# Decoder step: the sample tile's last mixing folded into four lanes, and the router's last prompt tiles fed without the shift

## The chip, the cores and the metric

The kernel runs on one core of one Trainium2 chip. The metric is device time in microseconds (us) of one execution. Three executions of the kernel before took 1709.33, 1714.53 and 1718.94 us; the median is 1714.53.

## The reference

One layer of a hybrid decoder for 1024 prompt tokens and 32 sample tokens (8 sequences of 4), model width 1024, all in f32. What matters for this change is the middle of the layer:

```python
merged = jax.nn.sigmoid(ga) * b_attn + jax.nn.sigmoid(gr) * b_lru
mix = merged @ p['w_out']
x = x + gt_a * _rms_norm(mix, p['g_post_mix'])
h2 = _rms_norm(x, p['g_pre_ffn']) * (1.0 + sc_f) + sh_f
f = _hier_moe(h2, p['w_router_group'], p['b_router_group'], ...)
x = x + gt_f * _rms_norm(f, p['g_post_ffn'])
```

`_rms_norm(x, g)` divides a row by the root of its mean square and multiplies by `g`. `_hier_moe` is a router and experts: `h2` times a router matrix of 36 columns (4 groups, 32 experts) plus a bias gives logits; the best group, and in it the best two of 8 experts, are chosen for each token; each expert computes `(silu(x @ w_gate) * (x @ w_up)) @ w_down` with two weights of 1024 x 512 and one of 512 x 1024 (2048 KB each), and the two results are added with the router's weights. `gt`, `sc` and `sh` come from a conditioning vector: one for the whole prompt, one for each of the 8 sample sequences.

## The kernel before, in words

The kernel is one program with an instruction list for each engine; every wait is written out as a semaphore. Tokens are split into three groups of columns (384, 384 and 288: the last has 256 prompt tokens and the 32 sample tokens) and nine tiles of rows, 0 to 7 of the prompt (128 rows) and 8, the sample tile (32 rows). Group g has the tiles 3g to 3g+2.

**Weights in a ring.** Steps of matrix products ("ga", "gr", "at", "lr" for the branches, "out" for the mixing) go through a ring of weights of 128 x 1024. SyncE (SP) loads one, ScalarE rounds it to the upper part (`round_weights`, L1186), VectorE subtracts to get the lower part (`split_weights`, L1645), and TensorE forms each product as three: upper x upper, upper x lower, lower x upper, in the form fp32r. The lower part is written over the raw weights.

**The last mixing.** The mixing of group g runs between the products of group g+1. That of the last group has nothing behind it: `mix(last, q)` for q = 0 to 7 (TensorE, definition above L2309, called behind the branches' products). A step takes two of eight slices of the contraction for one half of the 1024 columns: for each tile 2 x 3 products of 512 columns. Steps 0 to 3 make the left half, 4 to 7 the right half. VectorE meanwhile chooses experts for the six tiles of the groups before (`best`, L1767 to L1781, `choose`, L1786 to L1790), and in step 3 TensorE waits for that choice (`first_counts`) and for the order that VectorE makes from it (`early_places`, `first_order`), with which three experts are picked whose weights can be loaded at once (`eid0`, L1807).

**From the mix to the router.** For the last group, tile by tile: ScalarE squares the second half and takes a root (L1300, L1303); VectorE multiplies the mix by the gain (`last_half`, L1831), forms x1 (`last_x1`, L1839) and, with ScalarE's root of x1's squares (L1307, L1309), h2 (`last_h2`, L1846) and adds the shift B (L1847). TensorE turns h2 (`turn`, L2309), ScalarE copies it out of PSUM (`keep_turned`, L1237), TensorE multiplies it by the router matrix (`logits`), VectorE adds the bias (`keep_logits`, L1713) and chooses. In between TensorE multiplies matrices that nobody reads (`keep_warm`). The gains G1, A2 and B2 of the sample tile are rows of 1024 columns on 32 partitions, loaded by POOL (L917).

**From the router to the experts.** VectorE turns the choices into tables (L1868 to L1918): which token goes to which slot of 32 rows. When the first table is there, POOL gathers the token rows of two rounds from h2 in DRAM (`gather`, L925). A round of TensorE holds 128 slots, up to four experts side by side in four lanes of 32 rows: turn (L2428), gate, up, turn (L2463), down; all f32.

**Expert weights.** Three sets of buffers (gate, up, down) rotate. SP's queue is in order. It loads nine first weights (`first_weights`, L817) and then the rest (`expert_loads`, L841), each when the expert that had the buffer is done. Before the change the order around the router is:

```python
first_weights(0, ("gate", "up", "down"))
first_weights(2, ("gate",))
sp.wait_ge(step_done, STEP["out", GRP - 1, KC - 1] + 3)
first_weights(1, ("gate",))
... x1_store, h2_store of the last tiles
first_weights(1, ("up", "down"))
... waits for these stores and the turnings
first_weights(2, ("up",))
sp.wait_ge(tables, 4)
first_weights(2, ("down",))
```

Of the kernel before, what the change touches and what calls it, by code (L numbers as in the profile page):

```python
# [17 lines left out]
P = 128  # L18
# [45 lines left out]
XPAD = 3  # L64

# [28 lines left out]
LOW = 65536.0  # L94
assert [PLACE_RANK[n] for n in range(SETS)] == list(range(NE - SETS, NE))
# [80 lines left out]
def build(nc, I, O):  # L176
    ctx = ExitStack()
    with ctx:
# [143 lines left out]
        G1s, A2s, B2s = [at(n, [NS, D], m0[1] + i * D) for i, n in enumerate(("G1s", "A2s", "B2s"))]  # L322
# [79 lines left out]
        eprod0 = rtm("eprod0", [P, NE])  # L402
        rt, rt_end = 2 * big + KC * P, 2 * big + (RAW - 1 + UP) * KC * P
# [100 lines left out]
        idx_seen = sem("idx_seen")  # L504

        f_sum, f_pe, f_sq = sem("f_sum"), sem("f_pe"), sem("f_sq")
        y_added, y_pooled, st_out = sem("y_added"), sem("y_pooled"), sem("st_out")
# [4 lines left out]
        def row_sum(t):  # L512

            n = P if t < BLKS else NS
            if t in BY_PE:
                return ps[0:n, 2 * BY_PE.index(t) % 8:2 * BY_PE.index(t) % 8 + 2, :].rearrange("p h n -> p (h n)")
            return fy[0:n, t, 0, :]

# [22 lines left out]
        def tiles(g):  # L541

            return [(3 * g + j, j, P if 3 * g + j < BLKS else NS) for j in range(3)]

# [29 lines left out]
        def _(sp):  # L574
# [161 lines left out]
            def load_x(g):  # L736
# [3 lines left out]
                for t, j, n in tiles(g):  # L740
                    sp.dma_start(xh[j][0:n, :], I["x"][t * P:t * P + n, :]).then_inc(ld_xin, 16)

            def x1_store(t, j, n):
                sp.wait_ge(x1_ready, t + 1)
                sp.dma_start(x1_dram[t * P:t * P + n, :], x1[j][0:n, :]).then_inc(st_x1, 16)

            def h2_store(t, j, n):
                sp.wait_ge(h2_ready, t + 1)
                sp.dma_start(h2_dram[t * P:t * P + n, :], xh[j][0:n, :]).then_inc(st_h2, 16)
# [107 lines left out]
            sp.wait_ge(st_x1, 16 * TILES)  # L857
# [13 lines left out]
            for t in range(TILES):  # L871
                n = P if t < BLKS else NS
                if t in BY_POOL:
                    sp.wait_ge(y_pooled, BY_POOL.index(t) + 1)
# [8 lines left out]
        def _(pool):  # L883
# [1764 lines left out]
```

## Time and profile before

| | us |
|---|---|
| median of three runs (lowest, highest) | 1714.53 (1709.33, 1718.94) |
| the profiled execution, its own time | 1712.25 |
| span of the profiled execution | 1710.4 |
| TensorE busy | 1611.0 (94%) |
| VectorE, ScalarE, POOL busy | 753.6, 627.3, 128.1 |
| moved by DMA | 404.59 MB, mean 237 GB/s |

The profiled execution's own time is its span and 1.85 us around it. All times of the trace are counted from the start of the span. TensorE is shown as busy from the start of a product to its modelled end, so that two that follow each other overlap, and a plain f32 product is shown as two records; what a group of products costs is read from the starts. "What ended the idle time" of an engine is in brackets: idle us, then the work that it waited for.

### The profile page before, as it was taken

What the parts mean: (1) busy time and instruction counts of PE and PEld (TensorE: products, weight loads), DVE (VectorE), ACT (ScalarE), POOL (GpSimd) and SP (SyncE); (2) the same over time, 40 slices, a digit from 0 to 9 for tenths busy, and PEclk for the clock granted to TensorE, in tenths of its full rate; (3) what the DMA queues carried; (4) which work ended last, traced back from release to release, by engine and by line L of the source; (5) the groups of instructions that cost most, each with busy time, mean ns of one, the idle gap of its engine ahead of it and who ended that gap; (6) DMA issues with size and microseconds to landing.
All of it is one profiled execution on the core that took longest, in us unless ns stands there. A gap on an engine that the chain in (4) does not pass through costs nothing. (4 is left out here: it accounts for less than half of the span.)

```text
span 1710.4 us, 27124 instructions
## 1 busy us (share of the span) xinstructions
PE 1611.0 (94%) x11078; PEld 1159.1 (68%) x11078; DVE 753.6 (44%) x1402; ACT 627.3 (37%) x1191; POOL 128.1 (7%) x217
## 2 busy tenths in 40 slices
PE   6999988999999989999999999978998999999996
PEld 3889777888888889999999989762333333333343
DVE  3524347878888764453455455681000000000005
ACT  4525435665555663343444354321111111111112
POOL 0000011111111000000000030000000000000011
PEclk9999889999999999999999999999999999999998
DMA  9464561111111086373356564689999999999988
GB/s 375 167 199 143 172 199 50 54 42 53 54 54 53 27 297 216 127 271 124 124 185 234 185 196 159 247 321 376 417 392 428 428 424 424 406 406 392 408 323 313
DMA packets 96866, 404.59 MB, mean 237 GB/s; under 512 B 12215, under 2 KB 40151, under 8 KB 83800
## 3 DMA queue, kind: packets, MB, share of 16 engines
q1 hardware_dynamic: 84768, 380.23, 58.6%
q0 software_dynamic: 6960, 17.71, 2.7%
q10 hardware_dynamic: 5016, 4.93, 1.0%
q8 instruction: 88, 1.44, 0.3%
q14 instruction: 34, 0.28, 0.0%
HBM read 364.76 MB, written 44.32 MB: 239 GB/s over the span
## 5 line engine op out<-in xcount | busy, mean ns | idle before, releaser
L1186 ACT ACTIVATE wup<-wraw 128x1024 fp32r<-128x1024 f32 x120 | 126.7, 1059 | 272.2 <-PE ps L2002 234.4
L1645 DVE TENSOR_TENSOR wlow<-wraw,wup 128x1024 fp32r<-128x1024 f32 x120 | 146.8, 1224 | 158.9 <-ACT wup L1186 158.5
L2002 PE MATMUL ps<-wg,xT 128*32 128x512 f32 (+2 forms) x1072 | 156.1, 610 | 12.5 <-DMA wg<-w_gate 11.6
L2002 PE MATMUL ps<-wd,aT 128*32 128x512 f32 (+2 forms) x1072 | 148.5, 593 | 8.2 <-DMA wd<-w_down 6.8
L2002 PE MATMUL ps<-wu,xT 128*32 128x512 f32 (+2 forms) x1072 | 148.6, 594 | 4.2 <-DMA wu<-w_up 4.2
L2002 PE MATMUL ps<-h_up,wup 128*128 128x384 f32 (+1 forms) x384 | 126.1, 328 | 3.3 <-DVE wlow L1645 3.2
L2002 PE MATMUL ps<-h_up,wlow 128*128 128x384 f32 (+1 forms) x384 | 125.0, 326 | 0.0
L2002 PE MATMUL ps<-h_low,wup 128*128 128x384 f32 (+1 forms) x384 | 125.0, 325 | 0.0
L2002 PEld LDWEIGHTS ps<-wd,aT 128*32 128x32 f32 (+2 forms) x1072 | 47.1, 117 | 106.3 <-issue 104.6
L2002 PEld LDWEIGHTS ps<-wg,xT 128*32 128x32 f32 (+2 forms) x1072 | 44.9, 119 | 106.3 <-issue 103.1
L2002 PE MATMUL ps<-hp_up,wA_up 128*128 128x352 f32 x312 | 109.3, 350 | 0.6 <-DVE hp_low L1408 0.6
L1136 ACT ACTIVATE pp<-ps,ngm 128x256 f32<-128x256 f32 x128 | 59.5, 470 | 135.9 <-DVE skd L1530 120.4
L2002 PEld LDWEIGHTS ps<-wu,xT 128*32 128x32 f32 (+2 forms) x1072 | 46.0, 117 | 91.3 <-issue 89.4
L2002 PE MATMUL ps<-hp_up,wB_up 128*128 128x352 f32 x312 | 106.2, 340 | 1.6 <-ACT gB L1111 1.6
L2002 PE MATMUL ps<-hp_up,wA_low 128*128 128x352 f32 x312 | 102.3, 328 | 0.0
L2002 PE MATMUL ps<-hp_low,wA_up 128*128 128x352 f32 x312 | 102.2, 328 | 0.0
L2002 PE MATMUL ps<-hp_up,wB_low 128*128 128x352 f32 x312 | 100.8, 323 | 0.0
L2002 PE MATMUL ps<-hp_low,wB_up 128*128 128x352 f32 x312 | 100.7, 323 | 0.0
L1344 ACT ACTIVATE aT<-ps 128x512 f32<-128x512 f32 x20 | 11.9, 597 | 229.6 <-PE ps L2463 229.6
L1945 DVE TENSOR_TENSOR sgm<-sgm,ps 128x512 f32<-128x512 f32 x20 | 13.8, 688 | 168.4 <-ACT sgm L1336 168.4
L912 POOL COPY qst<-oT 64x128 f32<-64x128 f32 x128 | 57.8, 452 | 292.4 <-ACT oT L1165 288.0
L2002 PEld LDWEIGHTS ps<-h_up,wup 128*128 128x128 f32 x384 | 73.5, 192 | 4.5 <-issue 4.2
(402 smaller groups left out, 3291.9 us busy)
## 6 DMA issues: line engine op xcount, KB each, us to landing
wg<-w_gate SPq DMA_DIRECT2D x32, 2048.0 KB
wu<-w_up SPq DMA_DIRECT2D x32, 2048.0 KB, 15.9
wd<-w_down SPq DMA_DIRECT2D x32, 2048.0 KB, 14.3
wraw<-w_ga SPq DMA_DIRECT2D x24, 512.0 KB, 3.7
wraw<-w_gr SPq DMA_DIRECT2D x24, 512.0 KB, 3.6
wraw<-w_at SPq DMA_DIRECT2D x24, 512.0 KB, 3.5
wraw<-w_lr SPq DMA_DIRECT2D x24, 512.0 KB, 3.5
wraw<-w_out SPq DMA_DIRECT2D x24, 512.0 KB, 3.5
```

The source lines that it names most:

```text
L912: pool.tensor_copy(qst[half, u % 4, a, :], oT[half, u, i * P:(i + 1) * P]).then_inc(u_staged, 1)
L1136: act.activation(pp[:, s % 2, a, :], ps[:, 3 + s % 2, a * 2 * P:(a + 1) * 2 * P], ACT.Exp, bias=ngm[:, s % 2, a:a + 1], scale=SCALE, accum ...
L1186: act.activation(wup[n % UP][:, :, :], wraw[n % RAW][:, :, :], ACT.Copy).then_inc(w_rounded, 1)
L1344: act.activation(aT[:, :, :], ps[:, 6, :].rearrange("p (m c) -> p m c", c=P), ACT.Copy).then_inc(a_kept, 1)
L1645: V.tensor_tensor(wlow[n % RAW][:, :, :], wraw[n % RAW][:, :, :], wup[n % UP][:, :, :].bitcast(F32), ALU.subtract).then_inc(w_split, 1)
L1945: V.tensor_tensor(sgm[:, :], sgm[:, :], ps[:, 2, :], ALU.mult).then_inc(ch_moe, 1)
L2002: return pe.matmul(out, lhsT, rhs, start=start, stop=stop, skip_group_check=True)
```

## The change

The sample tile's part of the last mixing is computed as plain f32 from the raw weights, with the 32 rows in four lanes of 32 columns of the array: lane l makes the columns 128 l to 128 l + 127 of each half, and they land on partitions 32 l to 32 l + 31. The tile is then 128 x 256 instead of 32 x 1024, in x1, h2 and the gains. Row totals of squares are added over the lanes by a product with a matrix of zeros and ones (`same_row`). So that the raw weights live on, the lower parts of the last mixing go to buffers of their own. The two last prompt tiles are turned and multiplied by the router matrix before the shift B is added; B times the router matrix is computed once, ahead, and added to the bias (`br_shift`); B is added to h2 on VectorE afterwards. TensorE turns a tile before it multiplies the one before it, and is given fewer of the products that nobody reads. SP loads set 1's up weights together with its gate weights, stores the sample tile in four transfers, and issues the up weights of set 2 and the down weights of set 1 only when POOL has issued both first gathers (`pool_done`).

```diff
         G1p, A2p, B2p = [at(n, [P, D], t4 + i * D) for i, n in enumerate(("G1p", "A2p", "B2p"))]
-        G1s, A2s, B2s = [at(n, [NS, D], m0[1] + i * D) for i, n in enumerate(("G1s", "A2s", "B2s"))]
+        G1s, A2s, B2s = [at(n, [P, FD], m0[1] + 2 * KC * CW - (3 - i) * FD) for i, n in enumerate(("G1s", "A2s", "B2s"))]
+        wlow_last = [at(f"wlow_last{i}", [P, KC, P], m0[1] + i * KC * P, F32R) for i in range(UP)]
...
+                        sp.dma_start(lane_rows(x1_dram[SEQ:TOK, :], l), lane_part(x1[j], l)).then_inc(st_x1, 16)
+
+            def h2_store(t, j, n, ready=1):
+                sp.wait_ge(h2_ready, t + ready)
+                if t < BLKS:
+                    sp.dma_start(h2_dram[t * P:t * P + n, :], xh[j][0:n, :]).then_inc(st_h2, 16)
+                else:
+                    for l in range(LANES):
+                        sp.dma_start(lane_rows(h2_dram[SEQ:TOK, :], l), lane_part(xh[j], l)).then_inc(st_h2, 16)
 
             sp.wait_ge(proj_done, N_PROJ)
...
@@ -821,16 +860,17 @@
             first_weights(0, ("gate", "up", "down"))
             first_weights(2, ("gate",))
             sp.wait_ge(step_done, STEP["out", GRP - 1, KC - 1] + 3)
-            first_weights(1, ("gate",))
+            first_weights(1, ("gate", "up"))
             for t, j, n in tiles(GRP - 1):
                 x1_store(t, j, n)
-            for t, j, n in tiles(GRP - 1):
-                h2_store(t, j, n)
-            first_weights(1, ("up", "down"))
-            sp.wait_ge(st_x1, 16 * TILES)
-            sp.wait_ge(st_h2, 16 * TILES)
+            for j, ready in ((2, 2), (0, 5), (1, 5)):
+                h2_store(*tiles(GRP - 1)[j], ready)
+            sp.wait_ge(st_x1, 16 * (BLKS + LANES))
+            sp.wait_ge(st_h2, 16 * (BLKS + LANES))
             sp.wait_ge(h2_turned, 2 * TILES)
+            sp.wait_ge(pool_done, 1)
             first_weights(2, ("up",))
+            first_weights(1, ("down",))
             sp.wait_ge(tables, 4)
             first_weights(2, ("down",))
...
             for a, h, ts in ((0, 0, G1s), (1, 0, A2s), (0, 2, B2s)):
-                for b in range(NB):
-                    pool.dma_start(ts[NT * b:NT * (b + 1), :].rearrange("p (h n) -> p h n", h=2),
-                                   mod_dram[a, h:h + 2, 1 + b:2 + b, :].rearrange("h r n -> r h n").broadcast_to([NT, 2, 512])).then_inc(ld_samples, 16)
+                for l in range(LANES):
+                    for hh in range(2):
+                        pool.dma_start(ts[NS * l:NS * (l + 1), P * hh:P * (hh + 1)],
+                                       bc(mod_dram[a, h + hh, 1:1 + NB, P * l:P * (l + 1)].unsqueeze(1), (NB, NT, P))).then_inc(ld_samples, 16)
+            pool.dma_start(same_row[:, :], I["same_row"]).then_inc(ld_samples, 16)
 
             pool.wait_ge(tables, 1)
-            pool.wait_ge(st_h2, 16 * TILES)
...
             gather(1)
+            pool.sem_inc(pool_done, 1)
             pool.wait_ge(xg_used, 1)
             gather(2)
...
                 mix_piece(last, q)
+                if q == 5:
+                    act.wait_ge(lg_done, 3 * last)
+                    act.wait_ge(fold_pe, 1)
+                    act.activation(h2T[:, :, :], bc(ps[:, 7, SHIFT:SHIFT + KC].unsqueeze(2), (P, KC, P)), ACT.Copy).then_inc(rt_exp, 1)
             act.wait_ge(mix_sum, last + 1)
...
+                    act.wait_ge(fold_pe, 3)
+                    act.activation(tst[:, 3, j:j + 1], ps[:, 7, FOLD:FOLD + 1], ACT.Sqrt, bias=eps[:, :], scale=1.0 / D).then_inc(mix_root, 1)
+            def x1_square(j):
+                t, w = 3 * last + j, 2 * span(3 * last + j)
                 act.wait_ge(x1_ready, t + 1)
-                act.activation(junk[0:n, :], x1[j][0:n, :], ACT.Square, accum_out=tst[0:n, 4, j:j + 1]).then_inc(x1_sq, 1)
-                act.wait_ge(x1_sq, t + 1)
-                act.activation(tst[0:n, 5, j:j + 1], tst[0:n, 4, j:j + 1], ACT.Sqrt, bias=eps[0:n, :], scale=1.0 / D).then_inc(x1_root, 1)
...
-                dve.wait_ge(ld_xin, 48 * GRP)
-                V.scalar_tensor_tensor(x1[j][0:n, :], x1[j][0:n, :], tst[0:n, 3, j:j + 1], xh[j][0:n, :], ALU.mult, ALU.add).then_inc(x1_ready, 1)
+                dve.wait_ge(ld_xin, 16 * (BLKS + LANES))
+                V.scalar_tensor_tensor(x1[j][:, 0:w], x1[j][:, 0:w], tst[:, 3, j:j + 1], xh[j][:, 0:w], ALU.mult, ALU.add).then_inc(x1_ready, 1)
 
             def last_h2(j):
-                t, j, n = tiles(last)[j]
+                t, w = 3 * last + j, 2 * span(3 * last + j)
                 dve.wait_ge(x1_root, last + j + 1)
-                k(V.reciprocal(tst[0:n, 5, j:j + 1], tst[0:n, 5, j:j + 1]))
+                k(V.reciprocal(tst[:, 5, j:j + 1], tst[:, 5, j:j + 1]))
                 dve.wait_ge(x1_ready, t + 1)
-                k(V.scalar_tensor_tensor(xh[j][0:n, :], x1[j][0:n, :], tst[0:n, 5, j:j + 1], A2(t)[0:n, :], ALU.mult, ALU.mult))
-                V.tensor_tensor(xh[j][0:n, :], xh[j][0:n, :], B2(t)[0:n, :], ALU.add).then_inc(h2_ready, 1)
+                V.scalar_tensor_tensor(xh[j][:, 0:w], x1[j][:, 0:w], tst[:, 5, j:j + 1], A2(t)[:, 0:w], ALU.mult, ALU.mult).then_inc(h2_ready, 1)
+
+            def last_shift(j):
+                t, w = 3 * last + j, 2 * span(3 * last + j)
+                dve.wait_ge(h2_ready, TILES)
+                if t < BLKS:
+                    dve.wait_ge(h2_turned, 2 * t + 2)
+                V.tensor_tensor(xh[j][:, 0:w], xh[j][:, 0:w], B2(t)[:, 0:w], ALU.add).then_inc(h2_ready, 1)
 
             last_half(0)
             last_x1(0)
             last_half(1)
             last_x1(1)
             last_h2(0)
+            dve.wait_ge(fold_pe, 2)
+            k(V.tensor_tensor(br_shift[:, :], ps[:, 6, 0:NG + NE], brt[:, :], ALU.add))
             last_half(2)
             last_x1(2)
             last_h2(1)
             last_h2(2)
+            last_shift(2)
+            last_shift(0)
+            last_shift(1)
             keep_logits(last, 0, (6, 0))
             dve.wait_ge(lg_kept, 3 * last + 1)
...
+                    out, cols = ps[:, mix_bank(g, hf, j), :], slice(j * P, j * P + rows)
                     for kk in range(2):
                         k = 2 * kp + kk
+                        if t == BLKS:
+                            for l in range(LANES):
+                                ins = mm(ps[NS * l:NS * (l + 1), mix_bank(g, hf, j), 0:P], merged[g % 2][:, k, cols],
+                                         w_raw[:, kk, P * l:P * (l + 1)], k == 0, k == KC - 1)
+                            continue
                         mm(out, m_up[g % 2][:, k, cols], w_up[:, kk, :], k == 0, False)
                         mm(out, m_up[g % 2][:, k, cols], w_low[:, kk, :], False, False)
...
 
                 t, j, n = tiles(g)[j]
-                pe.wait_ge(h2_ready, t + 1)
+                pe.wait_ge(h2_ready, t + 1 + (t == BLKS))
+                if t == BLKS:
+                    pe.transpose(ps[:, at, 0:P], xh[j][:, part * P:(part + 1) * P], ident[:, :]).then_inc(h2_turned, 1)
+                    return
                 for k in range(4):
...
+            def row_totals(col, parts):
+
+                for i, s in enumerate(parts):
+                    ins = mm(ps[:, 7, FOLD + col:FOLD + col + 1], same_row[:, :], tst[:, s, 2:3], False, i + 1 == len(parts))
+                ins.then_inc(fold_pe, 1)
 
             def turn_along(g, o, q):
...
                 ins.then_inc(order_pe, 1)
+                for k in range(KC):
+                    ins = mm(ps[:, 7, SHIFT + k:SHIFT + k + 1], B2p[0:1, k * P:(k + 1) * P], ident[0:1, 0:1], True, True)
+                ins.then_inc(fold_pe, 1)
 
             for q in range(KC):
                 mix(last, q, {0: first_counts, 2: first_order} if q == 3 else {})
+            pe.wait_ge(rt_exp, 1)
             pe.wait_ge(rt_ready, 2)
             rank(0, 3 * last)
             pe.wait_ge(early_ready, 3)
-            keep_warm(44)
+            pe.wait_ge(mix_kept, 6 * last + 3)
+            pe.wait_ge(mix_sq, 6 * last + 3)
+            chunk_sum(ps[:, 6, 0:NG + NE], lambda k: h2T[:, k, :], lambda k: wr[:, k, :]).then_inc(fold_pe, 1)
+            pe.wait_ge(ld_samples, 16 * 3 * 2 * LANES + 16)
+            pe.wait_ge(mix_sq, 6 * last + 6)
+            row_totals(0, (0, 1))
+            keep_warm(14)
             pe.wait_ge(lg_kept, 3 * last)
-            for j in range(3):
+
+            def turn_last(j):
                 pe.wait_ge(mix_kept, 6 * last + 3 + j)
                 pe.wait_ge(mix_sq, 6 * last + 3 + j)
                 if j == 2:
                     pe.wait_ge(h2T_ready, 2 * 3 * last + 2)
                 turn(last, j, 0, (4, 0, 4)[j])
                 turn(last, j, 1, (5, 2, 5)[j])
-                keep_warm(5)
+
+            def logits_last(j):
                 if j:
                     pe.wait_ge(mix_kept, 6 * last + 4 + j)
                     pe.wait_ge(mix_sq, 6 * last + 4 + j)
                 if j == 2:
                     pe.wait_ge(lg_kept, 3 * last + 1)
                 logits(last, j, ((6, 1, 6)[j], 64 * (j // 2)), (h2T, h2Tb, h2T)[j])
-                if j < 2:
-                    keep_warm(6)
+
+            turn_last(0)
+            keep_warm(4)
+            pe.wait_ge(x1_sq, TILES)
+            row_totals(1, (4,))
+            turn_last(1)
+            logits_last(0)
+            turn_last(2)
+            logits_last(1)
+            logits_last(2)
```

## Rows read from the trace of the kernel before

**Rows 1.** The page: the chain that ended last, shares of the span by engine

```profile
PE 23%; DMA 8%; DVE 2%; issue 1%; ACT 0%; SPq 0%; POOLq 0%; POOL 0%; DVEq 0%; ACTq 0%
```

**Rows 2.** Chain of work in order of time (start us, us, what)

```profile
1148.90 4.72 DMA xg<-h_dram,slot_from
...
1448.42 16.29 DMA wu<-w_up
```

**Rows 3.** Busy us by stretch: the five engines, PE clock, DMA share, GB/s

```profile
1151.00:1152.00 1.00, 0.94 (x16) 0.91 (x16) 0.93 (x5) 0.00 (x0) 0.91 (x1) 1.00 0.82 188
1152.00:1153.00 1.00, 0.35 (x5) 0.11 (x2) 0.96 (x2) 0.00 (x0) 0.00 (x0) 1.00 0.64 164
1148.00:1170.00 22.00, 18.19 (x170) 7.84 (x172) 8.44 (x23) 3.07 (x4) 4.68 (x4) 1.00 0.71 257
1170.00:1464.00 294.00, 272.16 (x2008) 95.02 (x2000) 24.13 (x35) 37.39 (x59) 22.29 (x22) 0.98 1.00 418
1464.00:1640.00 176.00, 173.54 (x1272) 59.55 (x1272) 15.86 (x23) 24.04 (x38) 14.13 (x14) 1.00 0.98 402
```

**Rows 4.** Timeline of TensorE (start us, us, what), last mixing

```profile
1077.61 0.40 PE L2002 MATMUL ps<-wup,m_up 128*32 128x512 f32 x1
...
1079.00 0.39 PE L2002 MATMUL ps<-wup,m_up 128*128 128x512 f32 x1
...
1090.43 0.27 PE L2002 MATMUL ps<-ohs,ubf 128*128 128x32 bf16 x4 [1.49 <-DVE ohs L1790]
...
1093.63 0.50 PE L2002 MATMUL ps<-wup,m_up 128*128 128x512 f32 x1
...
1110.48 0.69 PE L2002 MATMUL ps<-ohs,ubf 128*128 128x32 bf16 x21
```

**Rows 5.** Timeline of TensorE: products in four lanes, 64 and 512 columns

```profile
234.96 1.10 PE L2002 MATMUL ps<-wslab,cE 128*32 128x64 f32 x64
...
1155.57 7.08 PE L2002 MATMUL ps<-wg,xT 128*32 128x512 f32 x64 [0.75 <-ACT xT L1330]
```

**Rows 6.** Timeline of TensorE's weight loads: router product, turning of 32 rows

```profile
1118.37 1.86 PEld L2002 LDWEIGHTS ps<-wr,h2T 128*128 128x128 f32 x16 [0.47 <-ACT h2T L1237]
...
1125.62 0.57 PEld L2309 LDWEIGHTS ps<-ident,xh 32*128 32x128 f32 x8 [0.21 <-issue]
```

**Rows 7.** Timeline of ScalarE: squares of the mix and of x1

```profile
1107.97 0.60 ACT L1300 ACTIVATE junk<-ps 128x512 bf16<-128x512 f32 x1 [8.71 <-PE ps L2002]
...
1111.97 1.04 ACT L1307 ACTIVATE junk<-x 128x1024 bf16<-128x1024 f32 x1
```

**Rows 8.** Timeline of VectorE, last mixing to the router

```profile
1092.32 0.24 DVE L1798 TENSOR_SCALAR lower<-key,kcol 128x32 bf16<-128x32 f32 x1
...
1113.88 1.28 DVE L1846 SCALAR_TENSOR_TENSOR xh<-x,tst,A2p 128x1024 f32<-128x1024 f32 x1
1115.20 1.23 DVE L1847 TENSOR_TENSOR xh<-xh,B2p 128x1024 f32<-128x1024 f32 x1
1116.35 0.67 DVE L1831 TENSOR_TENSOR x<-ps,G1s 32x512 f32<-32x512 f32 x1
...
1127.84 0.17 DVE L1767 COPY lg<-lg 128x8 f32<-128x8 f32 x1
```

**Rows 9.** Timeline of SyncE's queue: up weights of set 2

```profile
1130.73 0.34 SPq L817 DMA_DIRECT2D wu<-w_up  x1
```

**Rows 10.** Timeline of POOL: the first two gathers

```profile
1148.90 1.38 POOL L925 DMA_INDIRECT xg<-h_dram,slot_from  x1 [126.50 <-DVE slot_from L1918]
1150.58 1.32 POOL L925 DMA_INDIRECT xg<-h_dram,slot_from  x1 [0.30 <-issue]
```

**Rows 11.** Timeline of TensorE: two waits for expert weights

```profile
1324.66 3.11 PE L2002 MATMUL ps<-wg,xT 128*32 128x512 f32 x16 [4.41 <-DMA wg<-w_gate]
...
1384.06 2.37 PE L2002 MATMUL ps<-wd,aT 128*64 128x512 f32 x10 [2.24 <-DMA wd<-w_down]
```

**Rows 12.** Busy us by stretch, behind the longer of these waits

```profile
1326.00:1328.00 2.00, 2.00 (x15) 0.57 (x11) 0.00 (x0) 0.00 (x0) 0.00 (x0) 0.50 1.06 447
```

More of the change, by code:

```diff
@@ L64 @@
 XPAD = 3
+FD = D // LANES
 def worst_overflow():
@@ L94 @@
 LOW = 65536.0
+SHIFT = 384
+FOLD = 12 * NE
 assert [PLACE_RANK[n] for n in range(SETS)] == list(range(NE - SETS, NE))
@@ L543, in tiles, with span, prompt_width, low_part @@
             return [(3 * g + j, j, P if 3 * g + j < BLKS else NS) for j in range(3)]
+        def span(t):
+            return D // 2 if t < BLKS else FD // 2
+        def prompt_width(g):
+            return min(width(g), SEQ - CUT[g][0])
+        def low_part(n):
+            return wlow_last[n % UP] if n >= STEP["out", GRP - 1, 0] else wlow[n % RAW]
         def bank(key):
@@ L1299, in _ @@
                 act.wait_ge(step_done, STEP["out", last, KC - 1] + 1 + j)
-                act.activation(junk[0:n, 0:512], ps[0:n, mix_bank(last, 1, j), :], ACT.Square,
-                               accum_out=tst[0:n, 1, j:j + 1]).then_inc(mix_sq, 1)
-                act.wait_ge(mix_sq, 6 * last + 4 + j)
-                act.activation(tst[0:n, 3, j:j + 1], tst[0:n, 1, j:j + 1], ACT.Sqrt, bias=tst[0:n, 2, j:j + 1],
-                               scale=1.0 / D).then_inc(mix_root, 1)
-            for t, j, n in tiles(last):
-                act.wait_ge(x1_ready, t + 1)
-                act.activation(junk[0:n, :], x1[j][0:n, :], ACT.Square, accum_out=tst[0:n, 4, j:j + 1]).then_inc(x1_sq, 1)
-                act.wait_ge(x1_sq, t + 1)
-                act.activation(tst[0:n, 5, j:j + 1], tst[0:n, 4, j:j + 1], ACT.Sqrt, bias=eps[0:n, :], scale=1.0 / D).then_inc(x1_root, 1)
-                if j == 1:
-                    for part in range(2):
-                        keep_turned(last, 0, part, (4, 5)[part])
+                w = span(t)
@@ new lines, in x1_square, with x1_sqrt @@
+            def x1_square(j):
+                t, w = 3 * last + j, 2 * span(3 * last + j)
+                act.wait_ge(x1_ready, t + 1)
+                act.activation(junk[:, 0:w], x1[j][:, 0:w], ACT.Square, accum_out=tst[:, 4, j:j + 1]).then_inc(x1_sq, 1)
+            def x1_sqrt(j, total):
+                act.activation(tst[:, 5, j:j + 1], total, ACT.Sqrt, bias=eps[:, :], scale=1.0 / D).then_inc(x1_root, 1)
+            for j in range(2):
+                x1_square(j)
+                act.wait_ge(x1_sq, 3 * last + j + 1)
+                x1_sqrt(j, tst[:, 4, j:j + 1])
@@ L1313, in _ @@
+            keep_turned(last, 0, 0, 4)
+            x1_square(2)
+            keep_turned(last, 0, 1, 5)
+            act.wait_ge(fold_pe, 4)
+            x1_sqrt(2, ps[:, 7, FOLD + 1:FOLD + 2])
             for j in (1, 2):
@@ L2292, in mix @@
                 for t, j, rows in tiles(g):
-                    out, cols = ps[0:rows, mix_bank(g, hf, j), :], slice(j * P, j * P + rows)
+                    out, cols = ps[:, mix_bank(g, hf, j), :], slice(j * P, j * P + rows)
                     for kk in range(2):
                         k = 2 * kp + kk
+                        if t == BLKS:
+                            for l in range(LANES):
+                                ins = mm(ps[NS * l:NS * (l + 1), mix_bank(g, hf, j), 0:P], merged[g % 2][:, k, cols],
+                                         w_raw[:, kk, P * l:P * (l + 1)], k == 0, k == KC - 1)
+                            continue
                         mm(out, m_up[g % 2][:, k, cols], w_up[:, kk, :], k == 0, False)
```

82 lines of the change are left out of this document (55 added, 27 removed).

## The prediction

> **What bounds the kernel now.** I read the chain of work that ended last first. By its shares TensorE and DMA carry it [rows 1], and read in order of time it runs through three stretches. Up to the first gather of token rows it is a chain of small steps on TensorE, VectorE and ScalarE: POOL issues the gather at 1148.90 and it takes 4.72 us to land [rows 2]. From there to 1464.71 it goes through expert weights: the last link of that kind is an up load that takes 16.29 us from issue to landing [rows 2]. After that it is TensorE alone up to the last round.
>
> The busy times by stretch tell what such a long load means. From 1170 to 1464 the DMA engines are busy for a share of 1.00 at 418 GB/s, while TensorE is busy for 272 of 294 us; from 1464 to 1640 TensorE is busy for 173.5 of 176 [rows 3]. So for some 300 us the transfers are the bound, and what sets the end is when the stream of weights gets through. Just ahead of it, from 1148 to 1170, the DMA share is 0.71 [rows 3]: 6.4 us of DMA time idle. An earlier gather (I call the start of the first one T, 1148.90 now) moves the end only if the stream moves with it. That is the question of this change; the two parts of the answer follow.
>
> **Part 1: what the change takes from T.** *The mixing.* A step q of the last mixing has 18 products, six of them for the 32 sample rows: from 1077.61 to 1079.00, 1.39 us [rows 4]. After it there are 2 x 4 lanes of plain f32 at 128 columns. Such lanes run side by side: 64 records (8 sets of four lanes, each product shown as two records) take 1.04 us at 64 columns, 0.13 a set, and 7.08 us at 512 columns, 0.885 a set [rows 5]. At 128 columns a set lies between 0.13 and a quarter of 0.885, 0.22. I take 0.22, as the rows at 64 and 512 columns are in no proportion and the larger is the safer: 0.44 a step, 0.95 saved.
>
> In steps 0 to 2 that buys little. TensorE already stands still for 1.49 us in step 3, for VectorE's choice of experts (1088.94 to 1090.43) [rows 4]. VectorE's work there is one unbroken row that starts with the weights of step 0, so it moves by 0.95 only, to 1089.48. TensorE comes to that wait at 1085.93: the stall grows to 3.55 us. From there: second tile 1.40, sample tile 0.44, then the next VectorE result (its last step starts at 1092.32 and takes 0.24 [rows 8], less 0.95: 1091.6), and then the eight new one-row products that turn B. The trace has none with one row. Nearest are eight products with 128 x 128 weights, 1.86 us, and eight turnings of 32 rows, 0.57 [rows 6]. I take 1.86: the weights have 128 columns in both, and f32 products load them twice while turnings do so once. (The Trainium skill, "TensorE: Matmul & The Clock Gate", Step-by-step, has the time of a weight load go by its columns and not by its rows, which gives 1.86 too; the 32-row rows of this trace, at 0.07 a load against 0.12, speak for less. With 0.57, T and the forecast come 1.3 earlier.) Step 4 so starts at 1093.6, where it starts now (1093.63) [rows 4]. Steps 4 to 6 save 3 x 0.95, and the first tile of step 7 ends about **2.95 us earlier**.
>
> *The end of the stage*, counted from ScalarE's first square of the second half (1107.97) [rows 7]. Now x1's first square starts at +4.00 [rows 7], the first product of h2 at +5.91, and the last two tiles' choice at +19.87 [rows 8]. After the change:
> - TensorE ends the mixing at +1.55 (+2.51 now, less 0.95) [rows 4], counts ranks (0.55), makes the router's product of the shift (1.86) and the row totals (four records of 0.116, 0.46): +4.5. ScalarE, in order, waits there for the sample tile's total before x1's square: +4.85 in place of +4.00. VectorE had 0.2 us in hand, so h2 of the first tile starts at +6.5 and ends at +7.8.
> - VectorE now leaves out the addition of B there (1.23), and the sample tile's half and x1 shrink from 0.67 and 1.27 to some 0.25 and 0.40 (128 and 256 columns by the 0.67 for 512) [rows 8]. Tile two's h2 ends at +10.35, not +13.07.
> - TensorE: turning to +11.3, router product one to +13.15, sample turning, product two to +15.35, product three (0.7) +16.0. The sample's own router product is no shorter; it has the same form.
> - VectorE: sample h2 and its shift (0.7), two shifts of 1.23 to +13.7, logits and choice of the first tile (2.2), logits of the other two: +16.4. It and TensorE end together; a little off either buys nothing.
>
> +16.4 against +19.87 is 3.45. With 2.95, T comes **6.4 us earlier**, at 1142.5. The steps between that choice and the gather are unchanged.
>
> Costs that I set at nothing: nine more sample transfers on SP's queue, 0.34 us each [rows 9], issued while it waits for x1 and h2; POOL's 24 sample loads stay 24, plus one, and are issued right behind the second group's mixing, long before they are read; ScalarE's broadcast of B in step 5 (1024 columns, 1.04 us as its square of x1, while the engine idles 8.71 us ahead of +0 [rows 7]); Without that cover each would show in full. The last rows of h2 are ready at +13.7, 1118.7 on the clock, 24 us before T.
>
> **Part 2: what it gives back.** Two of the nine first weight loads, up of set 2 and down of set 1, are now issued ahead of the router's end, the later at 1130.73 [rows 9], and run while it works. Now SP holds them until both gathers are issued. They are 2 x 2048 KB: at 418 GB/s 10.0 us of transfers moved from before T, where the engines then stand idle, to behind T, where the stream is the bound. Every later weight load is queued behind them on SP. Against that they fill holes. POOL issues at T and T+1.68, the second for 1.32 [rows 10], so SP is let go at T+3.0, and I let data flow from T+4.0 on. The idle sum of 6.4 begins 0.9 us ahead of T (1148); from there, idle are 3.0 us up to T+2.1, and 0.18 and 0.36 of the next two by their shares, 0.82 and 0.64 [rows 3]: 3.5 us. Behind it nothing stops: with the down load of set 2 some 15 us of transfers are queued, and the next experts' loads come at about T+14, when the first gate products are done. So 10.0 - (6.4 - 3.5) = **7.1 us given back**.
>
> Sum: -6.4 + 7.1 = **+0.7 us**, no change. The profiled execution took 1712.25 us (span 1710.4) and would take 1713.0; the median of the three runs shown is 2.3 above it, so the forecast is 1714.53 + 0.7 = 1715.2. Ends of the terms: B's turnings -1.3, lane sets -0.7, the hole filling 1.0 either way, the tail of the stage 1.5 either way: 1711 to 1718.
>
> **Rivals.** *A, the stream is not the bound* that I take it for: the held loads vanish in idle DMA time and all 6.4 arrive: 1708.1. For it, TensorE is on the chain for most of those 300 us, and 1.00 is a share of packet time, not proof that nothing could be faster. Against it, 22 us of TensorE's idle time in that stretch, and the rate of 418 GB/s throughout.
>
> *B, slower: the clock.* The stall in step 3 grows to 3.55 us. Here an idle of 2.24 us left TensorE at a granted clock of 1.00, one of 4.41 us was followed by 0.50, that is 1.2 GHz, where 16 records took 3.11 us and not 1.77 [rows 11, 12]. That is 1.3 us lost on 16 records; the clock may stay low for more of them, 3.0 at most if it does so for 6 us. I take 2.0, all on the path as steps 4 to 7 are TensorE's: 1717.2. [...] The same page of the Trainium skill (HAM oscillation) has an idle engine fall to half rate and the products after the gap run slow, which is this rival; the trace agrees at 4.41 us.
>
> *C, the lanes do not run together* where all four share one set of weights: then the fold doesn't do what it says. Eight records of 128 columns in a row are as long as one set of 512, 0.885; a step grows by 0.4, T gains some 0.2 only, and 7.1 is given back: 1721.4. Against it, the same lane form in every expert round.
>
> **Chances.** Forecast 0.60, A 0.16, B 0.13, C 0.05, the rest (a table later, other contention) 0.06. The range takes A's value and most of B in: 1708 to 1720. A measurement of this kernel can tell about 0.5%, 8.6 us, from no change. No case alone crosses it: A lies 6.4 under, C 6.9 over. What crosses is a case with an error of its own: 0.08 faster, 0.07 slower, 0.85 the same.
>
> **What would show it.** In the profile after: sample products of a step in about 0.45 us; a hole of 3.5 us on TensorE in step 3, clock 1.00 behind it; first gather near 1142.5; a DMA share near nought for some 9 us ahead of it and 1.00 from T+4 on; the last long wait for weights still ends at about 1465. If that wait ends near 1458, A is right and the account of part 2 wrong. If the first gather is not 5 to 8 us earlier, part 1 is.

## The result and the profile after

Over 20 executions each, the kernel after took 1719.15 us (1713.78 to 1725.21) and the kernel before 1714.35 us (1709.33 to 1719.39); the ratio is 1.0032, 95% interval 1.0022 to 1.0042. So the change costs some 5 us, where +0.7 was forecast. That is inside the range of 1708 to 1720, by 0.9 us, and inside 0.5% of no change, but outside the noise: the sign is a small loss. The profiled execution took 1717.99 us, its span 1716.1 us, 5.7 more than before.

The chain of waits of the kernel after, around the first gather (start us, us, what), answers to [rows 2]:

```profile
1147.39 8.81 DMA xg<-h_dram,slot_from
...
1170.04 12.45 DMA wg<-w_gate
```

T is 1147.39, only 1.5 earlier, and 0.5 of this has come about ahead of the change (see the mark, below). The gather itself takes 8.81 us in place of 4.72.

Busy us by stretch, kernel after (PE, PEld, DVE, ACT, POOL; then PE clock, DMA share, GB/s), answers to [rows 3]:

```profile
1090.00:1096.00 6.00, 6.00 (x28) 4.95 (x32) 1.14 (x6) 0.00 (x0) 0.00 (x0) 0.50 0.31 109
1137.00:1149.00 12.00, 9.09 (x79) 7.31 (x77) 11.13 (x26) 0.93 (x1) 1.38 (x1) 0.85 0.02 7
1148.00:1170.00 22.00, 15.45 (x113) 6.84 (x114) 6.30 (x18) 2.58 (x4) 3.08 (x3) 0.77 0.89 355
1151.00:1168.00 17.00, 11.01 (x68) 3.92 (x72) 2.82 (x11) 1.88 (x2) 0.99 (x1) 0.70 1.00 423
1170.00:1464.00 294.00, 277.43 (x2024) 95.46 (x2020) 24.82 (x37) 36.52 (x58) 23.26 (x23) 0.97 1.00 418
1464.00:1640.00 176.00, 174.23 (x1296) 60.01 (x1290) 15.85 (x23) 24.73 (x39) 14.11 (x14) 1.00 0.98 403
```

Three things are to be seen. For 12 us ahead of the gather the DMA engines now do nothing (share 0.02). Behind it they are full, and the long stretch is full at 418 GB/s as before. And TensorE ran at half clock from 1090 to 1096, in step 3 of the last mixing, where before it had full clock.

Timeline of TensorE, kernel after, answers to [rows 4, 5]: a sample part of the mixing, the stall in step 3, the turnings of B and what follows, and the first round:

```profile
1084.36 0.64 PE L2083 MATMUL ps<-wraw,merged 128*32 128x128 f32 x16
...
1089.16 0.27 PE L2083 MATMUL ps<-ohs,ubf 128*128 128x32 bf16 x4 [2.56 <-DVE ohs L1861]
1089.35 3.57 PE L2083 MATMUL ps<-ident,B2p 1*128 1x1 f32 x16
1092.85 0.80 PE L2083 MATMUL ps<-wup,m_up 128*128 128x512 f32 x1
1093.44 0.63 PE L2083 MATMUL ps<-wlow_last,m_up 128*128 128x512 f32 x1
...
1095.71 0.82 PE L2083 MATMUL ps<-wraw,merged 128*32 128x128 f32 x16
1096.47 0.18 PE L2083 MATMUL ps<-lower,ubf 32*128 32x32 bf16 x1
1096.58 0.51 PE L2083 MATMUL ps<-wup,m_up 128*128 128x512 f32 x1
...
1156.24 1.97 PE L2543 MATMUL ps<-ident,xg 128*128 128x128 f32 x8 [5.39 <-DMA xg<-h_dram,slot_from]
1158.96 9.75 PE L2083 MATMUL ps<-wg,xT 128*32 128x512 f32 x64 [0.75 <-ACT xT L1398]
```

The first gate products take 9.75 us, not 7.08, as TensorE stood 5.39 us for the gather and came back at half clock (granted 0.70 in the mean from 1151 to 1168).

The end of the stage: ScalarE's and VectorE's timelines, kernel after, answer to [rows 7, 8]:

```profile
1109.08 0.60 ACT L1355 ACTIVATE junk<-ps 128x512 bf16<-128x512 f32 x1 [4.19 <-PE ps L2083]
...
1113.98 1.05 ACT L1367 ACTIVATE junk<-x 128x1024 bf16<-128x1024 f32 x1
```

```profile
1115.67 1.28 DVE L1917 SCALAR_TENSOR_TENSOR xh<-x,tst,A2p 128x1024 f32<-128x1024 f32 x1
...
1120.64 2.35 DVE L1924 TENSOR_TENSOR xh<-xh,B2p 128x1024 f32<-128x1024 f32 x2
...
1125.46 0.17 DVE L1838 COPY lg<-lg 128x8 f32<-128x8 f32 x1
...
1133.18 0.25 DVE L1962 TENSOR_SCALAR ohrank<-ps,row 128x32 bf16<-128x32 f32 x1 [0.94 <-PE ps L2083]
```

POOL and SyncE's queue, kernel after, answer to [rows 9, 10]:

```profile
1147.39 1.38 POOL L967 DMA_INDIRECT xg<-h_dram,slot_from  x1 [126.84 <-DVE slot_from L1999]
1149.08 1.32 POOL L967 DMA_INDIRECT xg<-h_dram,slot_from  x1 [0.31 <-issue]
```

```profile
1098.75 0.37 SPq L856 DMA_DIRECT2D wg<-w_gate  x1
...
1148.55 0.36 SPq L856 DMA_DIRECT2D wu<-w_up  x1
1149.69 4.89 SPq L856 DMA_DIRECT2D wd<-w_down  x2
```

The held up load is issued at 1148.55. That is 1.16 us behind T and ahead of the record of the second gather (1149.08), though the signal stands behind both in POOL's list: its flight lies beside both gathers.

The last long wait for weights ends, in the kernel after and then in the kernel before (timeline of TensorE):

```profile
1468.96 7.07 PE L2083 MATMUL ps<-wu,xT 128*32 128x512 f32 x64 [0.22 <-DMA wu<-w_up]
```

```profile
1465.04 7.07 PE L2002 MATMUL ps<-wu,xT 128*32 128x512 f32 x64 [0.92 <-DMA wu<-w_up]
```

So 3.9 of the 5.7 us have come about by then; the rest comes in the end stage, from there 247.1 us in place of 245.4.

### The profile page after: what moved, and what is told of

Read it like the earlier page. It is cut to its first block, busy times and chain, and to the rows that moved or that the text cites. A ratio compares the mean times of both kernels' runs of the same rounds, so it can differ in the third digit from the quotient of the medians.

```text
span 1716.1 us, 27261 instructions
## 1 busy us (share of the span) xinstructions
PE 1613.9 (94%) x11137; PEld 1160.3 (68%) x11137; DVE 750.1 (44%) x1403; ACT 627.1 (37%) x1192; POOL 127.5 (7%) x218
## 4 chain that ended last, share of the span: by engine, by line
PE 77%; DVE 9%; DMA 8%; ACT 3%; issue 2%; SPq 0%; DVEq 0%; ACTq 0%; POOLq 0%; POOL 0%
PE ps L2083 74%; DMA wd<-w_down 4%; PE ps L2543 1%; DMA wada<-w_ada 1%; DVE olst L1648 1%; PE ps L2295 1%; DVE mx L1596 1%; DMA wraw<-w_at 1%; DMA wlate<-w_ada 1%; DMA wg<-w_gate 1%; PE ps L2578 1%; DMA fy<-y_dram 1%; DMA xg<-h_dram,slot_from 1%; DVE xc L1638 0%; PE ps L2398 0%
## 5 line engine op out<-in xcount | busy, mean ns | idle before, releaser
L1713 DVE TENSOR_TENSOR wlow<-wraw,wup 128x1024 fp32r<-128x1024 f32 x112 | 136.9, 1224 | 153.8 <-ACT wup L1229 153.4
L2083 PE MATMUL ps<-wg,xT 128*32 128x512 f32 (+2 forms) x1072 | 159.6, 624 | 9.4 <-DMA wg<-w_gate 8.5
L2026 DVE TENSOR_TENSOR sgm<-sgm,ps 128x512 f32<-128x512 f32 x20 | 13.7, 687 | 168.7 <-ACT sgm L1404 168.7
## 6 DMA issues: line engine op xcount, KB each, us to landing
wu<-w_up SPq DMA_DIRECT2D x32, 2048.0 KB, 15.7
```

What stands on the lines that cost most here:

```text
L1713: V.tensor_tensor(low_part(n)[:, :, :], wraw[n % RAW][:, :, :], wup[n % UP][:, :, :].bitcast(F32), ALU.subtract).then_inc(w_split, 1)
L2026: V.tensor_tensor(sgm[:, :], sgm[:, :], ps[:, 2, :], ALU.mult).then_inc(ch_moe, 1)
L2083: return pe.matmul(out, lhsT, rhs, start=start, stop=stop, skip_group_check=True)
```

## Experiments

"The hold" is SP's wait for POOL's signal (`pool_done`) ahead of two weight loads. Executions differ ahead of the change as well, so every T is read from a mark that the change does not touch: the last product of the recurrent and attention branches. In the view of one tile (durations min/median/max, first and last start) before, and after:

```profile
L2002 PE MATMUL ps<-o_up,wlow x16: 289/296/297, 1050.3 to 1068.4; 128*128 128x288 f32 x16
```

```profile
L2083 PE MATMUL ps<-o_up,wlow x16: 289/295/297, 1049.8 to 1067.9; 128*128 128x288 f32 x16
```

The last start is the mark. In the table T and the end of the last long wait are counted from it; "slow" is the length of the stretch at half clock in step 3; "gather" is the flight of the first one; "DMA idle" is what the DMA shares of the 80 us from 30 to 110 behind the mark leave (in eight stretches of 10 us, 1 less the share). One profile each.

| kernel | median us | ratio to before | T | gather | slow | DMA idle | last wait |
|---|---|---|---|---|---|---|---|
| before | 1714.35 | 1 | 80.5 | 4.72 | none | 10.2 | 396.6 |
| after | 1719.15 | 1.0032 (1.0022–1.0042) | 79.5 | 8.81 | 6.8 | 15.8 | 401.1 |
| before, with the hold | 1720.91 | 1.0050 (1.0030–1.0069) | 80.5 | 9.78 | none | 18.1 | 402.8 |
| after, no hold | 1714.95 | 1.0007 (0.9991–1.0022) | 79.2 | 6.68 | 6.8 | 11.8 | 399.0 |
| after, longer hold | 1720.74 | 1.0042 (1.0025–1.0059) | 79.5 | at most 4.83 | 6.8 | 16.9 | 401.4 |
| after, B early | 1714.67 | 1.0013 (0.9996–1.0031) | 75.9 | 8.87 | 3.4 | 13.8 | 397.1 |
| no hold, B early | 1709.66 | 0.9965 (0.9951–0.9979) | 73.9 | 6.34 | none | 8.1 | 390.1 |
| the same, stores first | 1709.47 | 0.9972 (0.9958–0.9986) | 73.8 | 4.75 | none | 4.5 | 387.4 |
| after, kept warm | 1718.81 | 1.0022 (1.0008–1.0036) | 78.5 | 8.88 | 6.8 | 13.7 | 398.9 |
| before, one more input | 1714.80 | 0.9997 (0.9982–1.0012) | 80.6 | 4.71 | none | 9.9 | |

The ratios are the ones to compare: the medians of 6 to 12 executions are coarse, and a ratio and its medians differ by up to 2 us (B early with the hold: 2.2 us over the kernel before by the ratio, 0.3 by the medians). Single profiles are coarse too: in the kernel before with one more input, the products that end the last wait of the kernel before start at 397.8, 1.2 later, with the same instructions.

The last wait follows the DMA idle time. Against the kernel before, the hold alone adds 7.9 us of it and the last wait comes 6.2 later; the kernel after adds 5.6 and 4.5, the longer hold 6.7 and 4.8, no hold 1.6 and 2.4. In the three kernels with B early the last wait lies another 3 to 4 us lower than their idle time alone would have it, which is not explained.

**The hold alone, in the kernel before.** The theory is that the stream of weights is the bound, and the hold takes transfers out of it; the rival is that its price is what it does to the gather and to TensorE.

```diff
-            first_weights(1, ("up", "down"))
+            first_weights(1, ("up",))
...
+            sp.wait_ge(gathers_out, 1)
             first_weights(2, ("up",))
+            first_weights(1, ("down",))
```

(`gathers_out` is raised by POOL behind `gather(1)`.)

> The kernel before with one thing of the change: the up load of set 2 and the down load of set 1 wait on SP until POOL has issued both first gathers. Nothing else moves, so the first gather's start stays at about 1148.9. Theory S (the weight stream sets the end, and loads that are moved behind the gather push it): 10.0 us of transfers moved, some 2.5 to 2.9 us of idle DMA time filled, so 7 us slower than before, 1.004. Rival G (the stream is not the bound; what costs in the changed kernel is the longer flight of the gather, 8.8 us in place of 4.7, and TensorE's low clock after it): 4 to 6 us slower, with the wait for the gather longer and the last long weight wait not moved. Rival N (the held loads vanish in idle time): no change.

Measured: +6.5 us by the medians, last long wait 6.2 later. Busy us by stretch, in 50 us around the router, of this kernel and of the kernel before:

```profile
1122.00:1172.00 50.00, 36.33 (x332) 23.84 (x333) 28.44 (x99) 7.06 (x13) 3.69 (x3) 0.83 0.64 251
```

```profile
1122.00:1172.00 50.00, 40.11 (x386) 24.59 (x384) 29.41 (x100) 7.18 (x13) 4.68 (x4) 0.93 0.79 309
```

The share falls from 0.79 to 0.64, which is 7.5 us of transfers pushed behind this stretch: the size of the loss. The last wait, 300 us later, has moved by nearly the whole amount. But TensorE stands and runs slow here too (gather 9.78 us), and the next experts' load is issued 21.6 us behind T in place of 14.0, which could move the last wait as well. So the two are not apart by this kernel alone; the kernel with the longer hold parts them.

**The hold taken out of the kernel after.**

```diff
             sp.wait_ge(h2_turned, 2 * TILES)
-            sp.wait_ge(pool_done, 1)
             first_weights(2, ("up",))
```

> The changed kernel without the hold: the same two loads go out as soon as the h2 stores have landed. Theory S: the DMA engines work through from 1099 to the gather without a gap of more than 2 us, the first gather starts as in the changed kernel (1147.4), and the 7 us come back: 1712 us, 0.996 of the changed kernel and 0.999 of the kernel before. Rival G gives 4 us at most, if the gather is as short as before. Rival N: as the changed kernel, 1719.

Measured: 4.2 us less by the medians, level with before. That is between the 7 us of the one theory and the 4 us of the other and decides nothing. The hold's price is not wholly back, since without it SP is still late. Its queue in this kernel:

```profile
1112.90 0.34 SPq L856 DMA_DIRECT2D wu<-w_up  x1
...
1140.79 0.35 SPq L856 DMA_DIRECT2D wu<-w_up  x1
```

The load waits for h2's stores. They are issued 3 us later from the mark than before, as they now come behind the additions of B, and they land near 1140, 13.7 us behind the last issue (1127.08) in place of 6.7 (1124.01 to 1130.73 before): the up load of set 1 now stands ahead of them in the queue. The hold hid this second lateness.

**A longer hold**, until TensorE has read the first gathered rows.

```diff
-            sp.wait_ge(pool_done, 1)
+            sp.wait_ge(xg_used, 1)
```

> The changed kernel with a longer hold: the two loads wait until the first gather has landed and TensorE has turned it. The gather then flies alone, 4.7 us as before, and TensorE waits for it some 4 us less. Theory S: the gather's flight is beside the point; the DMA engines idle about 6 us more behind the gather, less the 1.5 us that POOL's third gather fills, so 3 to 5 us slower than the changed kernel. Rival G: 4 us faster than the changed kernel.

Measured: 1.6 us over the kernel after by the medians, with intervals that overlap; the last wait is 0.3 later. The theory had 3 to 5 us more, its rival 4 us less. The timeline of TensorE, then SP's queue:

```profile
1149.11 1.16 PE L2543 MATMUL ps<-ident,xg 128*128 128x128 f32 x8 [1.36 <-DMA xg<-h_dram,slot_from]
```

```profile
1151.12 0.36 SPq L856 DMA_DIRECT2D wu<-w_up  x1
```

The gathered rows are used 4.83 us behind T (1144.28), not 8.85: the slow gather was the held loads' doing. But they start 6.84 behind T, not 1.16. The next experts' load is issued 15.7 us behind T (1159.99), not 21.5. Four us won at the gather against 5.7 lost by the stream come to nought or a small loss. If the gather's delay and the late load behind it alone were the price, this kernel would have been the better one. What did not shrink is the idle time of the DMA engines, 16.9 us against 15.8. So the stream is the larger part, by less than the theory said.

**B turned ahead of the stall in step 3**, not behind it.

```diff
             def first_counts():
+                pe.wait_ge(lg_kept, 3 * last)
+                for k in range(KC):
+                    ins = mm(ps[:, 7, SHIFT + k:SHIFT + k + 1], B2p[0:1, k * P:(k + 1) * P], ident[0:1, 0:1], True, True)
+                ins.then_inc(fold_pe, 1)
                 pe.wait_ge(rt_ready, 1)
...
-                for k in range(KC):
-                    ins = mm(ps[:, 7, SHIFT + k:SHIFT + k + 1], B2p[0:1, k * P:(k + 1) * P], ident[0:1, 0:1], True, True)
-                ins.then_inc(fold_pe, 1)
```

> The changed kernel with B's eight one-row turnings put ahead of the wait for the first choice of experts in step 3, into TensorE's stall of 2.56 us, instead of behind it. Theory: they took 3.5 us there; the stall hides most of them, the first gather starts 2.5 to 3.5 us earlier (near 1144.5), the early weight loads too, and as the stream follows the gather the whole kernel is 2.5 to 3.5 us faster than the changed one, 1716. If the low clock behind the stall is what costs, it goes too, as TensorE is never idle for long: up to 2 us more. Rival: the loads' start does not matter and the stream stays: no change.

Measured: 4.5 us less than after by the medians, T 3.6 earlier from the mark. Timeline of TensorE:

```profile
1085.15 1.94 PE L2083 MATMUL ps<-ident,B2p 1*128 1x1 f32 x16
1087.78 0.28 PE L2083 MATMUL ps<-ohs,ubf 128*128 128x32 bf16 x4 [0.69 <-DVE ohs L1861]
```

The turnings fill the stall, of which 0.69 us is left, and cost 1.94 us at full clock, as against 3.57 in the kernel after. In this execution the clock still fell behind it, for 3.4 us (1087.83 to 1091.25).

**Both: no hold, and B early**, the two edits together.

> The changed kernel with both: no hold, and B's turnings ahead of the wait. The first gather starts near 1142.5 as with the turnings alone. Without the hold the last long wait for weights came 319.8 us after the gather's start, with it 321.2 to 321.6, before the change 316.1. Theory S with the buffers as a second limit (once all nine first loads have landed, no more can start until the gate products of the first round are done): 319.8 after 1142.5, so 1.5 us faster than the turnings alone and 2 us faster than the kernel before, 1712 to 1713. If no low clock follows the gather, 316 after 1142.5: 1709. Rival: the hold is needed once the gather is early, since the loads then run into it: no faster than the turnings alone, 1715.

Measured: 1709.66 us, ratio 0.9965, faster than before and after. Here the clock stayed up through step 3; of this kernel, by stretch:

```profile
1089.00:1097.00 8.00, 7.31 (x57) 5.64 (x56) 6.28 (x30) 2.54 (x5) 0.00 (x0) 1.00 0.61 215
```

Up to this point the kernel is the same as the last one, and differs from it in the profile only by the clock: 3.4 us at half rate there, none here. Step 4's first product, in this kernel and in the last one (timeline of TensorE):

```profile
1094.92 0.48 PE L2082 MATMUL ps<-wup,m_up 128*128 128x512 f32 x1
```

```profile
1091.65 0.50 PE L2083 MATMUL ps<-wup,m_up 128*128 128x512 f32 x1
```

It starts 23.6 us behind the mark (1071.3) here and 25.1 (1066.5) there. That prices this low stretch: 1.5 us. T is 2.0 apart (75.9 and 73.9), as the clock goes its own way behind the mixing too: the ranks keep VectorE waiting 0.94 us there and 0.26 here. From T to the last wait it is 316.2 us here, as in the kernel before (316.1): here all that T gains arrives.

**Stores first**: set 1's up load goes behind the stores of x1 and h2 as well.

```diff
-            first_weights(1, ("gate", "up"))
+            first_weights(1, ("gate",))
...
                 h2_store(*tiles(GRP - 1)[j], ready)
+            first_weights(1, ("up",))
```

> The last one with the up load of set 1 issued behind the stores of x1 and h2 instead of ahead of them, as in the kernel before. Theory: in the changed kernel the stores queue behind 10 MB of weights and land only near 1140, so that the two last loads cannot start before that; with the stores ahead they land some 5 us earlier, the DMA engines have no hole, and all loads are through before the gather. Gather alone again (4.7 us in place of 6.7 to 8.8), no low clock after it: 316 us from the gather to the last long wait, 1709, the fastest so far. Rival: the place of the stores does not matter, as the last one: 1712.

Measured: the same time within the interval (ratio 0.9972), though in the profile the last wait is another 2.7 us earlier. Around the router, by stretch, and TensorE's timeline at the gather:

```profile
1122.00:1172.00 50.00, 36.34 (x346) 21.78 (x345) 26.93 (x92) 4.62 (x8) 4.69 (x4) 0.88 0.90 350
```

```profile
1149.57 1.16 PE L2544 MATMUL ps<-ident,xg 128*128 128x128 f32 x8 [1.33 <-DMA xg<-h_dram,slot_from]
1151.48 7.07 PE L2083 MATMUL ps<-wg,xT 128*32 128x512 f32 x64 [0.75 <-ACT xT L1398]
```

The share is 0.90, hardly any weights fly beside the gather (share 0.50 in its flight, before 0.40), it takes 4.75 us, TensorE waits 1.33 us, and the first gate products take 7.07 us, as at full clock before. The stores land 62.1 us behind the mark, as before (62.3), and not at 67.0 as in the last kernel: so their lateness was for the most part the place of the up load. One profile is too little to claim the 2.7 us.

**Kept warm**: 16 products that nobody reads in the stall of the kernel after, to hold the clock.

```diff
             def first_counts():
-                pe.wait_ge(rt_ready, 1)
                 pe.wait_ge(mg_sig, len(SIGMOIDS))
                 pe.wait_ge(mg_out, len(SCALED))
+                keep_warm(16)
+                pe.wait_ge(rt_ready, 1)
```

> The changed kernel with 16 products that nobody reads in TensorE's stall of step 3, and B's turnings still behind the stall. It parts the two costs that moving the turnings took away together. If the low clock (0.50 from 1089.2 to 1096.1 in the changed kernel's profile) is the larger one: turnings in 1.9 us and not 3.5, second tile of the step 1.4 and not 2.6, the first gather 3 us earlier, near 1144.3, the kernel 1717 to 1718 in the median since only some executions have the low clock there. If the clock is beside the point: 1719 as the changed kernel.

Measured: 0.3 us under the kernel after, which is nothing, with T 1.0 earlier from the mark. By stretch:

```profile
1091.00:1092.00 1.00, 1.00 (x10) 1.00 (x10) 0.97 (x3) 0.00 (x0) 0.00 (x0) 1.00 0.96 369
1092.00:1093.00 1.00, 1.00 (x8) 1.00 (x7) 0.75 (x4) 0.00 (x0) 0.00 (x0) 0.61 1.02 383
1093.00:1099.00 6.00, 6.00 (x29) 4.22 (x30) 0.98 (x6) 1.64 (x3) 0.00 (x0) 0.50 0.10 30
```

The stall was down to 0.80 us and the clock came through it, but then fell at 1092.23, 1.3 us behind the start of B's turnings (1090.92) and while they ran, and stayed low for 6.8 us all the same. So here the fall came without a long idle, and filling the stall did not cure it. What did help was to have the turnings elsewhere.

**One more input.** From the last long wait to the end it is 246.6 to 247.7 us in every kernel made from the one after and in the kernel after, and 245.4 and 245.8 before and before with the hold. About a microsecond of it is the load of the results (10.3 to 11.1 us; before, and before with the hold, 9.35 to 9.38). A suspect was the added table `same_row`, which moves what lies in DRAM. The kernel before got it as an unused input.

```diff
+        "same_row": (q % NS == k % NS).astype(np.float32),
```

> The kernel before with only the 64 KB input that the change adds, never read. In the changed kernel and all kernels made from it the last loads of the results take 10.3 to 10.5 us and not 9.4, and the end from the last long weight wait is 1 to 2 us longer, 246.6 to 247.4 in place of 245.4. If that comes from where tensors lie in DRAM, it shows here: 1 to 1.5 us slower than the kernel before. If not, no change, 1714.4.

Measured: no change. The chain of waits shows the load of the results at its old length; this kernel first, then the kernel after:

```profile
1673.90 9.37 DMA fy<-y_dram
```

```profile
1674.43 10.52 DMA fy<-y_dram
```

The input is not the cause. What is stays open.

## Why the prediction was right, and where it was wrong

That 1719.15 lies in the range owes as much to its width as to the account: the sum's own ends were 1711 to 1718. Part 2 was right in kind and too high by 1.7 us, part 1 was 4.9 us off.

**The stream as the bound: right.** Rival A (all of an earlier T arrives, the held loads vanish) is out: the last wait ends at 1468.96, not near 1458, the hold alone costs 6.5 us, and the last wait moves with the idle time of the DMA engines. Of the 7.1 us given back, 5.4 show between T and the last wait (321.57 us against 316.14). The end stage adds 1.8, a term that the sum did not have; 1.1 of it is the load of the results above. -1.5, +5.4 and +1.8 make +5.7, by which the span grew. In between, two steps of that account were off and met each other: SP was let go at T+1.16 and not at T+3.0, and so data flowed earlier; but the gather then took 8.81 us, TensorE came late and slow, and the next experts' load was issued at T+21.5, not T+14 (1168.93 in the chain of waits; in the kernel with the stores first it is 1158.76, T+14.0). The DMA share from 1168 to 1171 was 0.59: the hole that was thought closed.

**Part 1: T 6.4 earlier was forecast, 1.5 measured** (1.0 from the mark). Of the 4.9 missing, 4.1 are there by ScalarE's first square (1109.08; the forecast has 1105.0):
- *The clock, some 3 us, is the step that failed.* VectorE's result came at 1089.16, forecast 1089.48. From there to step 4's first product (1096.58) the forecast has 4.1 us and the trace 7.4. The turnings of B took 3.5 us, not 1.86, the second tile 2.86 (1092.85 to 1095.71), not 1.40: both are twice their length, at a granted clock of 0.50. This is rival B, at its upper end of 3.0 us. It was given 0.13, for a stall of 3.55 us; the stall was 2.56, and the clock fell at 1089.31, 0.15 us behind its end. The Trainium skill, "TensorE: Matmul & The Clock Gate", HAM oscillation, says that the engine falls after idling and that what follows is slow; the trace agrees, and shows more: in the kernel kept warm the fall came during the turnings, not right behind an idle. What the rival lacked is the turnings: eight products of one column, right behind the stall, so that they ran at half clock. Whether they also bring the fall about is not shown. In this kernel and in the one with the longer hold it came 0.04 and 0.03 us ahead of the first turning, without the hold 0.2 us and kept warm 1.3 us behind its start. With them ahead of the stall, in three kernels, the low stretch was 3.4 us, none and none.
- *The order in step 3.* The forecast puts the turnings behind VectorE's next result. The kernel has them ahead of the second tile. By the forecast's own prices that comes to the same (1093.5 in place of 1093.6), but it is why they stand right behind the stall.
- *The lane sets, 1.0 us.* The sample part of a step takes 0.77 us (the period of a step went from 4.19 to 3.56, and 4.19 - 1.39 + 0.77 = 3.57), not 0.44. Steps 4 to 6 so give 0.33 less each. The forecast took a set's price from the long runs of one shape; here 16 records take 0.57 us from first start to the next product, 0.28 a set of four, above both ends of the stated bracket (0.13 and 0.22), and some 0.2 go at the two changes between the forms. The stall in step 3 was shorter for it (2.56 against 3.55), which is why steps 0 to 2 cost nothing more. Rival C (lanes one after the other, which has a set at 0.885 us) is out.
- *B's turnings at full clock: right.* 1.94 us with B early, forecast 1.86. A weight load of one row costs as much as one of 128 rows; the other end, 0.57 us from 32-row turnings, was wrong. The Trainium skill, "TensorE: Matmul & The Clock Gate", Step-by-step, has a load go by its columns and not by its rows; the trace agrees.

**The tail: right to a tenth.** x1's square at +4.90 (forecast +4.85), h2 at +6.59 (+6.5), the choice of the last two tiles at +16.38 (+16.4; before +19.87). Tiles turned ahead of the router products, the shift as a bias, and the narrow sample tile bring 3.5 us, as worked out.

**From the choice to the gather**, "unchanged" in the forecast, it took 21.93 us in place of 21.06 (with no hold and B early, 20.99). VectorE waits 0.94 us, not 0.28, for TensorE's ranks, which ran at low clock here (granted clock 0.53 from 1130 to 1135; before 0.91). The line of the kernel before (timeline of VectorE):

```profile
1134.82 0.25 DVE L1881 TENSOR_SCALAR ohrank<-ps,row 128x32 bf16<-128x32 f32 x1 [0.28 <-PE ps L2002]
```

4.1 + 0.9 is the missing 4.9 to a tenth.

**The whole.** The edits that were argued for are worth about 5 us: without the hold and with B early the kernel is 0.35% faster than before, T 6.6 earlier from the mark where 6.4 was forecast (1.9 more, as the stall hides the turnings, 1.3 less for the four lane parts from step 3 on, and 0.4 less in the tail, 16.78 us from the first square to the choice). The hold costs 4.2 and 5.0 us by the medians of the kernels after, with B late and early, and 6.5 in the kernel before; the place of eight tiny products costs 4.5 with the hold and 5.3 without (by the ratios some 3 and 7). The forecast had the hold right in kind and missed the place of the products.

## To carry to other kernels

Where a stream of loads is the bound, a wait that protects one small transfer is paid at the far end of the stream, by about the idle time that it makes; order the queue so that the small transfer finds it empty (stores first) before you hold loads back. Put products that barely use TensorE (one row, one column) where the engine would wait, ahead of the wait and not right behind it: behind it they took 3.5 us at half clock here, ahead of it 1.94, most of it hidden. And count T from a mark that the change can't touch, since executions differ by up to 6.5 us upstream.

## What was not expected of the hardware

- The clock fell in step 3 in all four profiles with the turnings behind the stall (2.56 us in three of them, 0.80 in the fourth), for 6.8 us each; with them ahead, it fell in one of three, for 3.4 us, behind an idle of 0.69 us that all three have. An idle of 2.24 us elsewhere left it up [rows 11]. What decides is open.
- A gather of 4.7 us alone takes 6.3 to 6.7 us beside loads that are under way, and 8.8 to 9.8 us beside two loads of 2048 KB, the first issued 1.1 to 1.2 us behind it and the second 2.3.
- A signal that stands behind two gathers in POOL's list let SP go 0.5 us ahead of the record of the second.
- The load of the results at the end takes 10.3 to 11.1 us in place of 9.4 in all profiles with the change, also in those of the two fastest kernels; its cause was not found.
